# RWKV stage on 64x64 blocks of the array, unrolled, with state steps and the next block's Gram products between the levels

## The chip, the cores and the metric

The kernel runs on one core of a Trainium2 chip. The metric is the device time of one execution in microseconds; the median of 3 runs of the kernel before is 1163.83 us.

The engines are TensorE (PE in the profile; its weight loads are PEld), VectorE (DVE), ScalarE (ACT), GpSimd (POOL) and SyncE (SP), which issues the loads. SBUF is the working memory of 128 partitions, PSUM has 8 banks (ps0 to ps7) of 512 float32 a partition.

## The reference, cut to what matters

One layer of a hybrid decoder on 512 tokens of width 1024: a token mixer with three groups of heads (RWKV-7, forgetting attention, stick-breaking attention), a cross-attention into 256 memory tokens, and a SwiGLU feed-forward part. The change touches only the RWKV-7 group: 6 heads of 64.

```python
def _rwkv7_scan(r, w, k, v, a, b):
    # S_t = S_{t-1}(diag(w_t) + a_t b_t^T) + v_t k_t^T, y_t = S_t r_t
    def step(S, inp):
        r_t, w_t, k_t, v_t, a_t, b_t = inp
        Sa = jnp.einsum('bhij,bhj->bhi', S, a_t)
        S = S * w_t[:, :, None, :] + Sa[..., None] * b_t[:, :, None, :] + v_t[..., None] * k_t[:, :, None, :]
        return S, jnp.einsum('bhij,bhj->bhi', S, r_t)
...
    y = _rwkv7_scan(r4, hs(decay), k4, v4, -kk, kk * a4.astype(jnp.float32))
```

Everything here is float32.

## The kernel before, in words

The kernel is written engine by engine: one instruction stream each, in the order of the code, with semaphores between them. Nothing schedules it. The stages follow each other: input projection (with weights split into a high and a low part, w_hi and w_lo, by GpSimd), the two kinds of attention, then the RWKV stage, the output projection, memory attention and feed-forward.

The RWKV stage doesn't walk token by token. It works in chunks of 64 tokens (CHUNK), two chunks in a block of 128, and four blocks, called turns (NT = 4). The 6 heads lie as 3 pairs c (APAIRS), the two heads g of a pair on partitions 0 to 63 and 64 to 127. In a turn:

- PRE (pre_bk, pre_r, pre_bkh, pre_a, L1505 to L1529) makes the decayed inputs AR (a and r), BK (b and k) and BKh from exponentials E (ScalarE, L1321).
- Four transposes on TensorE (L1066) bring a, b, k and v to tokens on partitions; ScalarE copies them out (L1331).
- Gram products: L1072 (b with a and r, into G1), L1079 (the lower part for Tm), L1085 (k with a and r, into G2). They are made for 128 x 128 tokens at once; the mask gram_mask clears what lies between the two chunks. VectorE masks them (L1541, L1557), adds ident (L1549, L1563) and makes the first inverse TT (L1564).
- L1091 makes the product of G2 and V for the right-hand side RHS.
- Five levels (LEVELS = 2, 4, 8, 16, 32) double the blocks of a triangular inverse: X = G1 with Tm (L1101), masked by VectorE with levm (L1574), then new Tm (L1108) and new TT (L1112), copied out by ScalarE (L1342). Each is a 128 x 128 product for each head, of which half is zero. The heads go in two groups of three, with banks of their own.
- TT times RHS gives WU (L1120, copy L1346). Then GT (L1125), the transfer matrices of both chunks (L1131, L1135, L1136), the state St (L1142, additions L1582 and L1590), the outputs (L1147, L1148, L1154) with the state laid out block-diagonally in Sbd (ScalarE, L1355).

Three turns run in a loop on each engine (Fori), the fourth is written out. A turn's state and outputs end before the next turn's transposes. Behind the stage come the head sums of the group norm (L1168) and the output projection. The masks are made by GpSimd at the kernel's start, between the splits of the first weight panels (L547, L551).

Of the kernel before, what the change touches and what calls it, by code (L numbers as in the profile page):

```python
# [12 lines left out]
P = 128  # L13
# [47 lines left out]
RW_STEPS = 7  # L61
RW_PRE = 6
# [21 lines left out]
def hybrid_block(nc, x, mem, norm_mix_pre, norm_mix_post, w_in, shift_mu, rwkv_w0, rwkv_w_up, rwkv_a0, rwkv_a_up,  # L84
# [4 lines left out]
    with ctx:  # L89
# [49 lines left out]
        grams = sb("gram_mask", [P, 2 * P], where=mix)  # L139
        lowm = sb("lowm", [P, P], where=mix)  # L140
        lowmT = sb("lowmT", [P, P], where=mix)
        levm = sb("levm", [P, len(LEVELS), P], where=mix)
        stack_id = sb("stack_id", [P, HD], where=mix)
# [38 lines left out]
        Rs = sb("Rs", [P, APAIRS, P], where=rw)  # L182
        ends = sb("ends", [P, 2, APAIRS, 1], where=rw)
        Vt = sb("Vt", [P, APAIRS, P], where=rw)
        Dg = sb("Dg", [P, 2, APAIRS, HD], where=rw)
        AR = sb("AR", [P, APAIRS, 2, P], where=rw)
        BK = sb("BK", [P, 2, APAIRS, P], where=rw)
        BKh = sb("BKh", [P, 2, APAIRS, P], where=rw)
        tokBK = sb("tokBK", [P, 2, AH, HD], where=rw)
        tokV = sb("tokV", [P, AH, HD], where=rw)  # L190
        G1 = sb("G1", [P, AH, 2 * P], where=rw)
        G2 = sb("G2", [P, AH, 2 * P], where=rw)
        Tm = sb("Tm", [P, AH, P], where=rw)
        TT = sb("TT", [P, AH, P], where=rw)
        X = sb("X", [P, AH, P], where=rw)
        RHS = sb("RHS", [P, AH, P], where=rw)
        WU = Tm
        GT = sb("GT", [P, APAIRS, P], where=rw)
        PT = sb("PT", [P, 2, APAIRS, P], where=rw)
        QS = sb("QS", [P, 2, APAIRS, HD], where=rw)  # L200
        St = sb("St", [P, 3, APAIRS, HD], where=rw)
        Sbd = sb("Sbd", [P, 2, APAIRS, P], where=rw)
# [261 lines left out]
        def _(sp_eng):  # L464
# [62 lines left out]
        def _(pool):  # L527
# [34 lines left out]
            fill(grams[:, :], 1.0)  # L562
            gv = grams[:, :].rearrange("p (a b j) -> p a b j", a=2, b=2)
            keep(gv[:, 0], [[CHUNK, 2], [1, CHUNK]], 0, -1, ALU.is_gt)
            keep(gv[:, 1], [[CHUNK, 2], [1, CHUNK]], 0, -1, ALU.is_ge)
            keep(gv, [[0, 2], [-CHUNK, 2], [0, CHUNK]], 0, 1, ALU.is_ge)
            fill(lowm[:, :], 0.0)
            keep(lowm[:, 0:P:2], [[-2, P // 2]], -1, 1, ALU.not_equal, 1.0)
            fill(lowmT[:, :], 0.0)
            keep(lowmT[:, :], [[-1, P]], 0, 1, ALU.not_equal, 1.0)  # L570
            keep(lowmT[:, 1:P:2], [[-2, P // 2]], 0, 1, ALU.not_equal, 1.0)
            fill(levm[:, :, :], 1.0)
            for n, m in enumerate(LEVELS):
# [3 lines left out]
                nb = P // (2 * m)  # L577
                v = levm[:, n, :].rearrange("p (b j) -> p b j", b=nb)
# [3 lines left out]
                keep(levm[:, n, :], [[-1, P]], 0, 1, ALU.not_equal, 1.0)  # L582
            for p in (2, 3):
                split(p, p % 2, p // 2)
            fill(stack_id[:, :], 0.0)
            keep(stack_id[:, :], [[-1, HD]], 0, 1, ALU.not_equal, 1.0)
            keep(stack_id[:, :], [[-1, HD]], -HD, 1, ALU.not_equal, 1.0)
# [47 lines left out]
        def level_steps(n, g, which):  # L635

            last = len(LEVELS) - 1
            if n < last:
                return 4 * n + 2 * g + which
            return 4 * n + g + 1  # L640
        N_TE = level_steps(len(LEVELS) - 1, 1, 2)
# [259 lines left out]
        def _(pe):  # L901
# [255 lines left out]
            with pe.Fori(0, NT - 1) as i:  # L1157
                rwkv_turn(i)
# [514 lines left out]
```

## Time and profile before

| | |
|---|---|
| median of 3 runs | 1163.83 us (1161.96 to 1168.35) |
| the profiled execution's span | 1160.8 us |
| PE, DVE, ACT, POOL busy in the span | 92%, 36%, 24%, 42% |
| RWKV stage, 314.6 to 498.1 us | 183.5 us |
| mean granted TensorE clock | 0.972 |

Busy time is the share in which an engine had an instruction under way. Matmuls overlap in the array, so a busy TensorE is not one at its peak; how closely records follow each other tells more. In a timeline a row can stand for several instructions (x10): its first number is the first start, its second the time until the last has ended. In brackets is how long the engine stood idle before it, and whose work ended that. The granted clock is 1.00 at 2.4 GHz and 0.50 at 1.2 GHz.

### The profile page before, as it was taken

The numbers are of one execution on the slowest core, as the hardware profiler recorded it, in microseconds if no ns is written. First come the engines' busy times: TensorE is split into PE (matmuls) and PEld (weight loads), VectorE is DVE, ScalarE is ACT, GpSimd is POOL, SyncE is SP. The second block draws the span as 40 slices with busy tenths as digits, with TensorE's granted clock in tenths as the row PEclk, the third lists the DMA queues.
The fourth block names the chain that finished last, engine by engine and source line by source line (L and its number), as shares of the span: only waits on it lengthen the run. The fifth ranks groups of instructions, "written<-read, shape, count | busy, mean of one in ns | idle before, by whom it ended". The sixth has DMA issues, their size and how long they took to land.

```text
span 1160.8 us, 14862 instructions
## 1 busy us (share of the span) xinstructions
PE 1069.9 (92%) x5717; PEld 861.7 (74%) x5717; DVE 416.5 (36%) x658; ACT 278.3 (24%) x575; POOL 487.2 (42%) x328
## 2 busy tenths in 40 slices
PE   6999997999998998999778988979999999999995
PEld 6788864555587887967766854878888888888884
DVE  4572036453354354262651033053333333320002
ACT  4111253445332332332311143132111111100101
POOL 7966633000000000027675620634666666666562
PEclk9999998999998999999999999989999999999998
DMA  7334211000000000003434310222333333322232
GB/s 214 90 91 107 76 51 57 1 1 1 1 1 1 0 0 0 2 19 109 145 119 136 91 55 1 87 59 74 107 91 91 107 91 91 108 91 91 91 98 83
DMA packets 101931, 79.16 MB, mean 68 GB/s; under 512 B 2656, under 2 KB 87936, under 8 KB 101888
## 3 DMA queue, kind: packets, MB, share of 16 engines
q1 hardware_dynamic: 100592, 73.85, 21.4%
q10 hardware_dynamic: 1296, 4.72, 1.2%
q8 instruction: 30, 0.49, 0.2%
q14 instruction: 13, 0.11, 0.0%
HBM read 76.46 MB, written 2.10 MB: 68 GB/s over the span
## 4 chain that ended last, share of the span: by engine, by line
PE 79%; DVE 9%; ACT 4%; POOL 3%; DMA 2%; issue 2%; DVEq 0%; ACTq 0%; POOLq 0%; SPq 0%
PE ps L425 11%; PE ps L426 11%; PE ps L427 11%; PE ps L455 7%; PE ps L457 7%; PE ps L456 7%; PE ps L1101 3%; PE ps L1112 2%; PE ps L1108 2%; PE ps L989 2%; PE ps L1027 2%; POOL w_lo L551 2%; PE ps L964 1%; DMA raw<-in_mem_wkv 1%; PE ps L696 1%
## 5 line engine op out<-in xcount | busy, mean ns | idle before, releaser
L547 POOL TENSOR_SCALAR w_hi<-raw 128x1024 fp32r<-128x1024 f32 (+2 forms) x135 | 153.0, 1133 | 637.4 <-PE ps L457 454.4
L551 POOL TENSOR_TENSOR w_lo<-raw,w_hi 128x1024 fp32r<-128x1024 f32 (+2 forms) x135 | 314.8, 2332 | 11.2
L425 PE MATMUL ps<-act_hi,w_hi 128*128 128x512 f32 (+1 forms) x632 | 236.9, 375 | 5.5 <-POOL w_lo L551 4.9
L426 PE MATMUL ps<-act_lo,w_hi 128*128 128x512 f32 (+1 forms) x632 | 235.8, 373 | 0.0
L427 PE MATMUL ps<-act_hi,w_lo 128*128 128x512 f32 (+1 forms) x632 | 235.7, 373 | 0.0
L425 PEld LDWEIGHTS ps<-act_hi,w_hi 128*128 128x128 f32 x632 | 119.1, 189 | 28.3 <-POOL w_lo L551 3.5
L427 PEld LDWEIGHTS ps<-act_hi,w_lo 128*128 128x128 f32 x632 | 119.1, 188 | 21.0
L426 PEld LDWEIGHTS ps<-act_lo,w_hi 128*128 128x128 f32 x632 | 119.1, 189 | 20.4
L393 DVE TENSOR_TENSOR ybuf<-ps,gain 128x512 f32<-128x512 f32 x24 | 16.4, 692 | 162.4 <-ACT junk_f L374 117.0
L455 PE MATMUL ps<-w_hi,act_hi 128*128 128x512 f32 (+2 forms) x192 | 71.4, 372 | 2.4 <-DVE act_lo L824 1.4
L457 PE MATMUL ps<-w_hi,act_lo 128*128 128x512 f32 (+2 forms) x192 | 69.8, 363 | 0.0
L456 PE MATMUL ps<-w_lo,act_hi 128*128 128x512 f32 (+2 forms) x192 | 69.8, 363 | 0.0
L457 PE MATMUL ps<-w_hi,a_lo 128*128 128x512 f32 x176 | 69.6, 396 | 0.0
L456 PE MATMUL ps<-w_lo,a_hi 128*128 128x512 f32 x176 | 69.6, 395 | 0.0
L455 PE MATMUL ps<-w_hi,a_hi 128*128 128x512 f32 x176 | 69.6, 395 | 0.0
L886 DVE TENSOR_TENSOR a_lo<-ftmp,a_hi 128x512 f32 (+1 forms) x22 | 56.5, 2570 | 19.6 <-ACT a_hi L868 19.6
L884 DVE TENSOR_TENSOR ftmp<-ps,ftmp 128x512 f32<-128x512 f32 x22 | 15.2, 692 | 88.2 <-PE ps L427 88.2
L455 PEld LDWEIGHTS ps<-w_hi,act_hi 128*128 128x128 f32 x192 | 36.2, 189 | 9.4 <-DVE act_lo L824 2.2
L868 ACT ACTIVATE a_hi<-ftmp 128x512 f32 (+1 forms) x22 | 14.0, 634 | 122.0 <-DVE ftmp L884 122.0
L456 PEld LDWEIGHTS ps<-w_lo,act_hi 128*128 128x128 f32 x192 | 36.2, 188 | 5.7 <-issue 0.7
L457 PEld LDWEIGHTS ps<-w_hi,act_lo 128*128 128x128 f32 x192 | 36.2, 188 | 5.1
L456 PEld LDWEIGHTS ps<-w_lo,a_hi 128*128 128x128 f32 x176 | 33.1, 188 | 8.1
(280 smaller groups left out, 1608.0 us busy)
## 6 DMA issues: line engine op xcount, KB each, us to landing
raw<-in_ffn_w_gu SPq DMA_DIRECT2D x44, 512.0 KB, 3.8
raw<-in_ffn_w_down SPq DMA_DIRECT2D x22, 512.0 KB, 3.7
raw<-in_w_in SPq DMA_DIRECT2D x21, 512.0 KB, 3.8
raw<-in_mem_wkv SPq DMA_DIRECT2D x16, 512.0 KB, 3.8
raw<-in_w_out SPq DMA_DIRECT2D x8, 512.0 KB, 3.7
raw<-in_mem_wq SPq DMA_DIRECT2D x8, 512.0 KB, 3.8
raw<-in_mem_wo SPq DMA_DIRECT2D x8, 512.0 KB, 3.7
xt<-in_x SPq DMA_DIRECT2D x4, 512.0 KB, 7.3
```

What stands on the lines that cost most here:

```text
L425: nc.tensor.matmul(o, hi, a_hi_[:, k, at:at + n], start=(k == 0), stop=False)
L426: nc.tensor.matmul(o, hi, a_lo_[:, k, at:at + n], start=False, stop=False)
L427: last = nc.tensor.matmul(o, lo, a_hi_[:, k, at:at + n], start=False, stop=(k == KT - 1))
L455: nc.tensor.matmul(o, xh, hi, start=(nth == 0 and kk == 0), stop=False)
L456: nc.tensor.matmul(o, xh, lo, start=False, stop=False)
L457: last = nc.tensor.matmul(o, xl, hi, start=False, stop=(nth == pairs - 1 and kk == 1))
L547: nc.gpsimd.tensor_scalar(w_hi[slot][:, 0:n], raw[slot][:, 0:n], 1.0, 1.0, ALU.mult, ALU.mult)\
L551: nc.gpsimd.tensor_tensor(w_lo[slot][:, 0:m], raw[slot][:, 0:m], w_hi[slot][:, 0:m].bitcast(F32), ALU.subtract).then_inc(sig("panel_split" ...
L886: V.tensor_tensor(a_lo[:, bass.ds(f, 1), :], ftmp[:, 2 + b, :].unsqueeze(1), a_hi[:, bass.ds(f, 1), :].bitcast(F32), ALU.subtract).then_in ...
L989: mm(ps[bank][:, 0:NJ[j]], qk[half(h), 2 * APAIRS + CH // 2 + h // 2, P * j:P * j + P], qk[half(h), 2 * APAIRS + h // 2, P * j:T], start=T ...
L1027: last = mm(ps[b][:, P * (j2 - j):NJ[j]], (ntri if j2 == j else nones)[:, :], sp[h % 2][:, OJ[j2]:OJ[j2] + NJ[j2]], start=False, stop=(j2 ...
L1101: last = mm(ps[g][:, P * c:P * c + P], G1[:, 3 * g + c, 0:P], Tm[:, 3 * g + c, :], start=True, stop=True)
```

## The change

The RWKV stage is written anew on all three engines, with the same arithmetic in the same type:

- All products are made for each chunk apart, 64 x 64, with chunk 0 on partitions 0 to 63 and chunk 1 on 64 to 127. G1, G2, Tm, TT and X shrink from 128 to 64 columns for each head, and nothing between chunks is computed. In each product the matmuls alternate between the two chunks (or the two heads of a pair), so that neighbours use different quarters of the array.
- The six heads of a level go as one group: one mask on VectorE and one copy for Tm and for TT on ScalarE, each of 384 columns, where there were two.
- The state is kept as 64 x 64 for each head (St0 to St3), so the block-diagonal copies Sbd and PT and their additions go. PQ takes the transfer matrices and what is added to the state in one VectorE operation for each chunk.
- The state steps and outputs of turn i stand between the levels of turn i + 1. The Gram products of turn i + 1 stand in level 4 of turn i. The transposes stand one by one in the levels 0 to 3. AR, BK, G1, G2, tokV and ends have two buffers.
- The four turns are written out without a loop.
- The masks are 64 wide, made by GpSimd on 64 partitions in one tile, chunk_masks, and copied to the other 64 by a DMA on SP's queue, ahead of the loads of the Q panels.

```diff
+            def by_chunk(bank, lhs, rhs, width, heads=range(AH)):
+                for n, hh in enumerate(heads):
+                    for ch in range(2):
+                        last = mm(ps[bank][half(ch), width * n:width * n + width], lhs[half(ch), hh, :], rhs[half(ch), hh, :],
+                                  start=True, stop=True)
+                return last
...
+            def turn_pe(i):
+                more = i + 1 < NT
+                level_x(i, 0)
+                toks(0, i)
+                if i:
+                    pe.wait_ge(sig("rw_pq"), 2 * i)
...
+                    state_step(i - 1, 0)
+                level_t(i, 0)
+                pe.wait_ge(sig("rw_tok"), 4 * i + 1)
+                gram(i, 0, 3, 1, "rw_g2m")
...
+            def transfers(i):
+                dve.wait_ge(sig("rw_dg"), 2 * i + 3)
                 for ch in range(2):
+                    dve.wait_ge(sig("rw_pqm"), 2 * i + ch + 1)
+                    V.tensor_tensor(PQ[:, ch], ps[2 + 2 * ch][:, 0:AW].rearrange("p (a c n) -> p a c n", a=2, c=APAIRS),
+                                    Dg[:, ch], ALU.add).then_inc(sig("rw_pq"), 1)
...
+            sp_eng.wait_ge(sig("half_masks"), 1)
+            sp_eng.dma_start(chunk_masks[CHUNK:P], chunk_masks[0:CHUNK]).then_inc(sig("masks_both"), 16)
```

TensorE in the levels, before. A row is a run of equal matmuls, with the bank that it writes and its size; L1101 is X, L1108 and L1112 are the new Tm and TT:

```order
L1101 MATMUL ps0<-Tm,G1 128x128 x3
...
L1101 MATMUL ps1<-Tm,G1 128x128 x3
...
L1108 MATMUL ps2<-X,TT 128x128 x3
L1112 MATMUL ps4<-TT,X 128x128 x3
...
L1108 MATMUL ps3<-X,TT 128x128 x3
L1112 MATMUL ps5<-TT,X 128x128 x3
```

And in the change, levels 1 and 2 of turn 1 (L1075 is by_chunk; L1104 a state step and L1113, L1116, L1122 the outputs of turn 0; L1058 a Gram product, L1050 a transpose):

```order
L1075 MATMUL ps0<-Tm,G11 64x64 x12
L1104 MATMUL ps4<-St1,PQ 64x64 x6
L1058 MATMUL ps3<-AR1,BK1 64x128 x6
L1075 MATMUL ps1<-X,TT 64x64 x12
L1075 MATMUL ps2<-TT,X 64x64 x12
L1050 MATMUL ps4<-ident,AR1 128x128 x3
...
L1075 MATMUL ps3<-tokV1,G21 64x64 x12
L1113 MATMUL ps4<-G10,WU 64x64 x2
L1116 MATMUL ps4<-G20,tokV0 64x64 x2
```

Two groups of three heads became one group of 12 small matmuls, and between X and the T products now stands work of other steps and of the turn before.

VectorE from a turn's end on, before (PT, GT, St, Y are the transfer, output and state additions):

```order
L1582 TENSOR_TENSOR PT<-ps2,Dg 64x3x64 x2
L1582 TENSOR_TENSOR PT<-ps3,Dg 64x3x64 x2
L1586 TENSOR_TENSOR GT<-ps7,Rs 128x384
L1590 TENSOR_TENSOR St<-ps4,QS 128x192 x2
...
L1595 TENSOR_TENSOR Y<-ps6,Y 128x3x128
...
L1537 COPY St<-St 128x192
L1541 TENSOR_TENSOR G1<-ps4,gram_mask 128x512
```

And in the change, from level 4 of turn 0 to level 0 of turn 1:

```order
L1636 TENSOR_TENSOR G11<-ps3,chunk_masks 128x384
L1648 TENSOR_TENSOR Tm<-ps4,chunk_masks 128x192
L1648 TENSOR_TENSOR Tm<-ps3,chunk_masks 128x192
L1651 TENSOR_TENSOR Tm<-Tm,chunk_masks 128x384
L1653 TENSOR_TENSOR G11<-G11,chunk_masks 128x6x64
L1712 COPY WU<-ps1 128x384
L1658 TENSOR_TENSOR TT<-G11,chunk_masks 128x384
L1682 TENSOR_TENSOR PQ<-ps2,Dg 128x384
L1682 TENSOR_TENSOR PQ<-ps4,Dg 128x384
L1687 TENSOR_TENSOR GT<-ps0,AR0 128x3x64
L1687 TENSOR_TENSOR GT<-ps1,AR0 128x3x64
L1667 TENSOR_TENSOR X<-ps0,chunk_masks 128x384
```

The next turn's masks and additions now stand ahead of this turn's WU, PQ and GT, and the state addition comes behind the next turn's first X.

## Rows read from the trace of the kernel before

**Rows 1.** The page's first part: busy time, share and instructions of each engine.

```profile
PE 1069.9 (92%) x5717; PEld 861.7 (74%) x5717; DVE 416.5 (36%) x658; ACT 278.3 (24%) x575; POOL 487.2 (42%) x328
```

**Rows 2.** Windows, turns two and four, and all four's sum; columns: us, busy by engine, clock.

```profile
360.48:407.65 47.17, 43.09 (x374) 40.33 (x372) 20.39 (x42) 16.19 (x36) 0.00 (x0) 0.92 0.00 0
...
453.14:498.10 44.96, 39.98 (x373) 36.85 (x370) 17.98 (x36) 15.83 (x33) 0.00 (x0) 1.00 0.00 1
sum 183.50, PE 165.74 PEld 153.81 DVE 80.19 ACT 64.62 POOL 0.00; mean PE 41.44 PEld 38.45 DVE 20.05 ACT 16.16 POOL 0.00
```

**Rows 3.** The chain, one level: start us, us, engine and line.

```profile
378.11 1.51 PE ps L1101 x12
...
380.36 0.67 PE ps L1112 x6
...
382.37 1.51 PE ps L1101 x12
```

**Rows 4.** Groups by shape in turn two: busy us, mean ns of one.

```profile
L1574 DVE TENSOR_TENSOR X<-ps,levm 128x384 f32<-128x384 f32 x10 | 5.6, 558 | 12.5 <-PE ps L1101 12.5
...
L1342 ACT ACTIVATE Tm<-ps 128x384 f32<-128x384 f32 x8 | 3.9, 491 | 7.7 <-PE ps L1108 7.7
...
L1590 DVE TENSOR_TENSOR St<-ps,QS 128x192 f32<-128x192 f32 x2 | 0.7, 352 | 2.1 <-PE ps L1142 2.1
```

**Rows 5.** TensorE's timeline, the transfer matrices in 64x64: start us, us until the last end.

```profile
397.17 0.61 PE L1131 MATMUL ps<-tokBK,Tm 64*64 64x64 f32 x10
397.57 0.22 PE L1135 MATMUL ps<-Tm,tokBK 64*64 64x64 f32 x1
397.62 0.22 PE L1131 MATMUL ps<-tokBK,Tm 64*64 64x64 f32 x1
397.63 0.22 PE L1135 MATMUL ps<-Tm,tokBK 64*64 64x64 f32 x1
397.68 0.22 PE L1131 MATMUL ps<-tokBK,Tm 64*64 64x64 f32 x1
...
397.80 0.28 PE L1135 MATMUL ps<-Tm,tokBK 64*64 64x64 f32 x2
397.92 0.28 PE L1136 MATMUL ps<-tokV,tokBK 64*64 64x64 f32 x2
...
400.07 0.28 PE L1136 MATMUL ps<-tokV,tokBK 64*64 64x64 f32 x2
...
400.29 0.88 PE L1142 MATMUL ps<-St,PT 128*128 128x64 f32 x6
```

**Rows 6.** The timeline of turn two, handoffs to TensorE; idle time in brackets.

```profile
367.94 1.35 DVE L1541 TENSOR_TENSOR G<-ps,gram_mask 128x256 f32<-128x256 f32 x3
...
369.34 2.83 PE L1091 MATMUL ps<-tokV,G 128*128 128x64 f32 x12 [2.00 <-DVE G L1541]
...
395.55 0.49 ACT L1346 ACTIVATE Tm<-ps 128x384 f32<-128x384 f32 x1 [0.35 <-PE ps L1120]
...
396.10 1.14 PE L1125 MATMUL ps<-G,Tm 128*64 128x128 f32 x12 [0.58 <-ACT Tm L1346]
```

**Rows 7.** Windows, three stretches with their granted clock (the last number but two).

```profile
348.60:355.40 6.80, 6.22 (x103) 5.74 (x103) 2.06 (x6) 1.15 (x3) 0.00 (x0) 1.00 0.02 5
365.70:369.10 3.40, 1.64 (x14) 1.15 (x10) 2.84 (x7) 0.00 (x0) 0.00 (x0) 1.00 0.00 0
369.10:376.00 6.90, 6.66 (x31) 6.66 (x32) 4.60 (x10) 2.25 (x5) 0.00 (x0) 0.51 0.00 0
```

**Rows 8.** GpSimd's timeline in the opening.

```profile
36.05 1.19 POOL L534 TENSOR_SCALAR_AFFINE_SELECT stack_id<-stack_id 128x64 f32<-128x64 f32 x2
```

**Rows 9.** The chain in the opening.

```profile
42.82 0.51 POOL w_lo L551
...
52.27 2.41 POOL w_lo L551
54.73 0.50 PE ps L425
```

More of the change, by code:

```diff
@@ L60 @@
 SMALL_LOADS = 16 * 12
-RW_STEPS = 7
-RW_PRE = 6
 def panel_run(eng, first, count, unroll, body):
@@ L138, in hybrid_block @@
         reset = sb("reset", [P, T], where=mix)
[L139 to L143, printed above, removed]
+        chunk_masks = sb("chunk_masks", [P, 2 + 2 + len(LEVELS) + 1, CHUNK], where=mix)
+        grams = chunk_masks[:, 0:2, :]
+        lowm, lowmT = chunk_masks[:, 2, :], chunk_masks[:, 3, :]
+        levm = [chunk_masks[:, 4 + n, :] for n in range(len(LEVELS))]
+        eye = chunk_masks[:, 4 + len(LEVELS), :]
         att = ExitStack()
@@ new lines, in gram, with lower @@
+            def gram(i, g, bank, b, sem):
+                for c in range(APAIRS):
+                    for ch in range(2):
+                        now = slice(CHUNK * ch, CHUNK * ch + CHUNK)
+                        last = mm(ps[bank][half(ch), P * c:P * c + P].rearrange("p (a n) -> p a n", a=2),
+                                  BK[i % 2][half(g), b, c, now], AR[i % 2][half(g), c, :, now], start=True, stop=True)
+                last.then_inc(sig(sem), 1)
+            def lower(i, g, bank):
+                for c in range(APAIRS):
+                    for ch in range(2):
+                        now = slice(CHUNK * ch, CHUNK * ch + CHUNK)
+                        last = mm(ps[bank][half(ch), CHUNK * c:CHUNK * c + CHUNK], AR[i % 2][half(g), c, 0, now],
+                                  BK[i % 2][half(g), 0, c, now], start=True, stop=True)
+                last.then_inc(sig("rw_nm"), 1)
@@ new lines, in level_t, with state_step @@
+            def level_t(i, n):
+                pe.wait_ge(sig("rw_x"), len(LEVELS) * i + n + 1)
+                if n == 0:
+                    pe.wait_ge(sig("rw_t2"), i + 1)
+                else:
+                    pe.wait_ge(sig("rw_te"), TURN_TE * i + 2 * n)
+                if n < LAST:
+                    by_chunk(1, TT, X, CHUNK).then_inc(sig("rw_tm"), 1)
+                by_chunk(2, X, TT, CHUNK).then_inc(sig("rw_tm"), 1)
+            def state_step(i, ch):
+                n = 2 * i + ch
+                for c in range(APAIRS):
+                    for g in range(2):
+                        last = mm(ps[4][half(g), HD * c:HD * c + HD], PQ[half(g), ch, 0, c, :], St[n % 4][half(g), c, :],
+                                  start=True, stop=True)
+                last.then_inc(sig("rw_sm"), 1)
@@ L1157, in _ @@
-            with pe.Fori(0, NT - 1) as i:
-                rwkv_turn(i)
-            rwkv_turn(NT - 1)
+            pe.wait_ge(sig("masks_both"), 16)
+            pe.wait_ge(sig("rw_in"), 1)
+            gram(0, 0, 4, 0, "rw_g1m")
+            gram(0, 1, 3, 0, "rw_g1m")
+            pe.wait_ge(sig("rw_g1"), 1)
+            lower(0, 0, 4)
+            pe.wait_ge(sig("rw_g1"), 2)
+            lower(0, 1, 3)
+            for i in range(NT):
+                turn_pe(i)
+            pe.wait_ge(sig("rw_pq"), 2 * NT)
@@ L1364, in _ @@
+            act.wait_ge(sig("stick_pv"), CH)
+            for which in range(3):
+                decay(0, which)
+            for i in range(NT):
+                turn_act(i)
+            y_out(NT - 1, 0)
+            y_out(NT - 1, 1)
             for c in range(APAIRS):
```

555 lines of the change are left out of this document (294 added, 261 removed).

## The prediction

> **What bounds the kernel now.** I read first the busy line of the page: TensorE works in 92% of the span [rows 1]. The change touches one stretch, the RWKV stage, which is four turns (blocks of 128 tokens). The windows, one per turn, give its size: from 314.6 to 498.1 us, 183.5 us in all, 45.0 to 47.2 us a turn, and in a turn TensorE is busy 41.4 us, VectorE 20.1, ScalarE 16.2 and GpSimd not at all [rows 2]. So the stage is paced by TensorE. The chain shows it at its finest: one level of the triangular inverse is nothing but matmul pieces, 1.51 us for the X product and then pieces of about 0.67 us without a gap, 4.26 us from one level's start to the next [rows 3]. That is 36 records (6 heads x 3 products, and a float32 matmul leaves two records) at 0.118 us. The masks on VectorE (0.56 us) and the copies on ScalarE (0.49 us) lie beside it [rows 4], because the six heads are worked as two groups of three, and one group's matmuls run while the other's result is masked or copied. Everything behind 498.1 us hangs on the end of this stage.
>
> **What a small tile costs.** The new code does nearly all of this on 64x64 quarters of the array, so its price per record is the term that decides. The old kernel has one place of that kind [rows 5]. Where one quarter alone is fed, records start 0.058 us apart: two of L1135 from 397.80, then L1136 at 397.92. Where two quarters have work, they run at once: L1135 and L1131 start at 397.57, 397.62, 397.63 and 397.68, 0.03 us from one to the next, each line's records keeping their 0.058. The whole block of 72 records takes 3.12 us (397.17 to 400.29), 0.043 each, since the old order feeds one quarter six or twelve records in a row. The second quarter joins only when about three records of the first are left, so the array looks only a few records ahead. The new order gives one matmul to one quarter and the next to the other, within that reach. I take 0.029 us a record, with bounds 0.0146 (four quarters at once) and 0.058 (none at once). A record that streams 128 columns takes twice that, 0.056 on two quarters. Full 128x128 transposes stay at 0.112, as six records in 0.67 us [rows 3]. Between a quarter-mode record and a full-mode one lie 0.17 us (last L1136 at 400.13, L1142 at 400.29) in place of 0.06: 0.1 us for each change of mode.
>
> **One level, new.** X product: 24 records x 0.029 = 0.70 us, 0.22 for the last to land [rows 5], 0.05 to wake VectorE, 0.56 for the mask (same 384 columns as before, but now for all six heads), 0.1 to restart TensorE: the T products start at 1.63. Their first half again takes 0.92, 0.05, then the ScalarE copy 0.49 and 0.06: the next X product can start at 3.15. Wake-ups are from the rows in which an engine waited: 0.05 us from VectorE's end (367.94 + 1.35) to L1091 at 369.34, and 0.06 from ScalarE's 396.04 to L1125 at 396.10 [rows 6]. TensorE issues 72 records x 0.029 = 2.1 us of that. The level is no longer TensorE's own pace but a round trip over three engines, with about 0.9 us free between X and T. Into that hole and behind T the change puts other work. Behind T it is not hidden, since T ends at 3.03.
>
> **One full turn, new,** by the order of the rows of after. TensorE's work: 288 matmuls on 64 columns = 576 records x 0.029 = 16.8 us; 36 on 128 columns = 72 records x 0.056 = 4.0; 12 transposes = 24 x 0.112 = 2.7; 8 changes of mode = 0.8. Sum 24.3 us, against 41.4 busy now. By levels, start to start: levels 0 and 1 with transposes, a state step and a Gram half each 4.2; level 2, which holds the product with V and both output groups, 5.9, with two waits of 0.25 on its own results; level 3 with two transposes 4.0; level 4 with Gram, lower part, solution, transfer matrices and GT up to the next level 0: 10.0. Sum 28.3 us. So about 4.0 us remain in which TensorE waits: the masks and copies that the fill doesn't cover, 0.9 for the copy of WU, and some 1.3 at the turn's end, where GT's two additions stand ahead of the next X product. VectorE has 21 operations x 0.56 and 8 x 0.35 [rows 4], 14.6 us, ScalarE some 10: neither becomes the bound. The old tail of each turn (state steps, their copies into Sbd, the output products, each behind the other) now lies under the next turn's levels, and the wait of 2.00 us for the Gram masks ahead of L1091 [rows 6] goes, because the next block's Gram products are made before this block's end.
>
> **The whole stage.** Prologue (first block's Gram and lower products with four masks and two additions, nothing to hide them) 4.4 us. Turn 0 has no earlier state to carry, 96 records and a wait less, but then shows some mask waits: 25.0. Turns 1 and 2: 56.6. The last turn and what follows it (two state steps with a VectorE addition each, and two output groups, all in series) 32.6. Sum 118.6 us.
>
> **The clock.** The granted clock falls to 0.50 (1.2 GHz) at 369.1, behind a stretch in which TensorE was busy for 1.64 us of 3.40 [rows 7]. From 348.6 to 355.4 it worked on parts of the array only and kept 1.00, 2.4 GHz [rows 7], so small tiles alone don't lower it. In the new turn the gaps at the end (0.9 and 1.3 us, close together) are of that kind. At half clock a turn of 28.3 us would be 51 (24.3 doubles, less the mode changes), so each microsecond at half costs 0.45. I put in three falls of 3.4 us, 4.6 us in all; as in the stage of now, they may be more or fewer. **Stage 123.2 us, a gain of 60.3.**
>
> **The opening.** The masks are half as wide and made on half of the partitions, and stack_id is gone. Most of that is hidden: GpSimd then waits for the panel to be used. But stack_id's selects took 1.19 us of GpSimd at 36.05 [rows 8], between two splits of panels for which TensorE later waited: the chain goes over w_lo for 0.51 us at 42.82, and again over w_lo at 52.27 up to L425 at 54.73 [rows 9]. With 1.19 us less ahead both waits go or shrink: the first is worth its 0.51, the second what is left of the 1.19 at most; I take 1.0 us for both. The new copy of the masks to the other half of the partitions (160 KB) stands on SP's queue ahead of the Q panels; behind it wait only loads that a full slot holds back, and its readers wait at 311 us. The 512 KB loads land in 3.8 us on the page. I cost it at nothing; if SP's queue stood still for that whole time once, 4 us would be lost at most, and nothing reads a gain from it.
>
> **Sum.** 60.3 + 1.0 = 61.3 us. Against the profiled span of 1160.8 that gives 1099.5; the median of the runs is 3.0 us above the span, so 1102.5 us. A difference of 0.5% (5.8 us) is about what a measurement of this kernel can tell from none.
>
> By the Trainium skill, page "TensorE: Matmul & The Clock Gate", section "Part 3: Packing small matmuls", matmuls on tiles of different groups start about 4 ns apart, so all four quarters would run at once. The trace never shows more than two for long. By that rule the 96 records of the transfer matrices and GT, which alone use four quarters, would take 1.4 us in place of 2.8 in a turn, and the sum would be 1096.9.
>
> **Rivals.**
> (a) The four quarters do run at once, or the waits that I count at the turn's end are covered: 96 records x 0.0146 less in four turns, 5.6 us, and no falls of the clock, 4.6: 1092.
> (b) The clock stays low. If half of the new stage runs at half clock, the stage is 118.6/(1 - 0.45 x 0.5) = 153 us and the kernel 1132. For it: TensorE now stops for a mask or a copy in every level. Against it: the gaps of a level are under 0.2 us with the fill, and the Gram and small-tile stretches of now kept 1.00.
> (c) The other side: quarters on opposite corners don't run at once when fed in turn, and a record takes 0.058. Then a turn has 576 x 0.058 + 72 x 0.112 + 3.5 = 45 us of TensorE work, and with some 3 us of waits 48; the stage is 4.4 + 44 + 96 + 46 = 190 us and with the falls of the clock 195, and the kernel 1174, slower than now. It decides from 0.055 us a record on (118.6 grows by 2.5 for each 0.001). Against it: the interleaved starts at 397.57 to 397.68 and a mean of 0.043 even in the unfavourable order. The same end is reached if over 80% of the stage is at half clock.
> (d) Unrolling: the turn is now straight code of some 336 matmuls, read once. If instruction loads lag behind the short records by 1 to 1.5 us a few times a turn, 5 to 20 us are lost: 1108 to 1122. The three turns of the old loop read the same code again, so the trace says little for or against.
>
> **Chances.** My forecast with its own range 1094 to 1112: 0.60. (a) 0.10, (b) at 1112 to 1150: 0.13, (d) 0.10, (c) 0.06, and 0.01 for within 0.5%. The range 1088 to 1132 takes in (a), (d), the nearer half of (b) and both ends of the tile price that still give two quarters at once. Faster by over 0.5%: 0.93; within: 0.01 plus the tail of (b), 0.02; slower: 0.05.
>
> **What the profile would show.** Right: the stage (from the first Gram product to the first of the head sums) in 118 to 128 us; four turns near 28; the X and T products with 0.029 us from record to record; masks at 0.56 and copies at 0.49 us as before; VectorE's mask waiting for L1075, and TensorE waiting for the mask only briefly; clock at 1.00 but for a few short falls at the turns' ends; behind the stage everything as now, 60 us earlier. Wrong: records 0.058 apart within a product; long stretches at 0.50; gaps on TensorE that end with no releaser; or a level 4 of over 12 us, which would mean that VectorE's queue (Gram masks, additions, the copy of WU, then the transfers) is the turn's real path.

## The result, and the profile after

The changed kernel takes 1084.63 us (median of 4 runs, 1082.1 to 1088.38), the kernel before on the same chip 1162.89 (1160.64 to 1168.35). The ratio is 0.932, with a 95% interval of 0.928 to 0.936. The forecast was 1102.5 with 1088 to 1132: right in direction, and too small a gain, 61.3 us where the profiled spans differ by 77.1 (1160.8 and 1083.7). Of the 17.9 us between 1102.5 and 1084.6 the spans account for 15.8; the other 2.1 come from the median, which lies 0.9 us above the profiled span and not 3.0.

The page after, first part: busy us, share of the span, instructions.

```profile
PE 1000.1 (92%) x6869; PEld 795.2 (73%) x6869; DVE 393.0 (36%) x609; ACT 250.3 (23%) x511; POOL 481.0 (44%) x325
```

TensorE works 70 us less [rows 1], with a fifth more records. Windows of the stage after, in the columns of [rows 2]: the prologue, turn 0, turn 1 (turn 2 reads the same, 24.88), the last turn with its tail up to the first product of the head sums, and the two stretches at half clock.

```profile
314.06:318.15 4.09, 2.19 (x50) 1.77 (x49) 2.79 (x7) 0.00 (x0) 0.00 (x0) 0.93 0.00 0
318.15:343.18 25.03, 22.70 (x565) 20.79 (x565) 13.19 (x29) 8.56 (x18) 0.00 (x0) 0.87 0.01 3
343.18:368.05 24.87, 22.41 (x660) 20.79 (x661) 13.26 (x30) 9.23 (x20) 0.00 (x0) 1.00 0.02 4
...
392.93:423.74 30.81, 26.24 (x709) 23.54 (x709) 8.84 (x21) 8.70 (x20) 0.00 (x0) 0.94 0.01 3
317.60:324.40 6.80, 6.25 (x91) 5.80 (x92) 1.61 (x4) 1.88 (x4) 0.00 (x0) 0.50 0.01 2
420.00:426.80 6.80, 6.25 (x56) 4.22 (x53) 2.77 (x4) 1.95 (x3) 0.00 (x0) 0.50 0.01 2
```

The stage takes 423.74 - 314.06 = 109.7 us where it took 183.5 [rows 2]: 73.8 us of the 77.1. The forecast was 123.2.

| part of the stage | forecast, us | after, us |
|---|---|---|
| prologue | 4.4 | 4.1 |
| turn 0 | 25.0 | 25.0, of it 6.2 at half clock |
| turns 1 and 2 | 56.6 | 49.75 |
| last turn and tail | 32.6 | 30.8, of it 3.7 at half clock |
| falls of the clock, apart from these | 4.6 | 0 |

Turn 1 by levels, each from its X product to the next level's, in the same columns:

```profile
343.18:346.74 3.56, 3.56 (x97) 3.33 (x99) 0.92 (x2) 1.21 (x3) 0.00 (x0) 1.00 0.00 0
346.74:350.56 3.82, 3.82 (x106) 3.59 (x102) 2.87 (x6) 1.53 (x4) 0.00 (x0) 1.00 0.03 6
350.56:356.07 5.51, 5.38 (x170) 5.10 (x171) 2.58 (x7) 2.82 (x7) 0.00 (x0) 1.00 0.01 3
356.07:359.61 3.54, 3.36 (x84) 2.82 (x80) 1.02 (x2) 2.08 (x5) 0.00 (x0) 1.00 0.02 5
359.61:368.05 8.44, 6.29 (x217) 5.96 (x217) 5.87 (x13) 1.58 (x4) 0.00 (x0) 1.00 0.02 5
```

The forecast had 4.2, 4.2, 5.9, 4.0 and 10.0: every level is shorter, most of all the last. In levels 0 and 1 TensorE has no idle time at all; nearly all of its 2.46 us of waiting in the turn lie in level 4. The timeline after shows level 0 and the end of level 4 (start us, us until the last end, then engine, line, count; idle time in brackets):

```profile
343.18 0.92 PE L1075 MATMUL ps<-Tm,G 64*64 64x64 f32 x24 [1.44 <-DVE GT L1687]
344.02 0.55 PE L1050 MATMUL ps<-ident,z 128*128 128x128 f32 x3
...
344.50 0.56 PE L1104 MATMUL ps<-St,PQ 64*64 64x64 f32 x12
344.90 0.87 PE L1075 MATMUL ps<-X,TT 64*64 64x64 f32 x24
345.60 0.80 PE L1075 MATMUL ps<-TT,X 64*64 64x64 f32 x21
...
346.19 0.32 PE L1058 MATMUL ps<-AR,BK 64*64 64x128 f32 x1
346.19 0.28 PE L1075 MATMUL ps<-TT,X 64*64 64x64 f32 x3
...
364.98 0.34 PE L1141 MATMUL ps<-tokBK,WU 64*64 64x64 f32 x8 [0.71 <-issue]
365.12 0.33 PE L1145 MATMUL ps<-WU,tokBK 64*64 64x64 f32 x8
365.23 0.33 PE L1149 MATMUL ps<-tokV,tokBK 64*64 64x64 f32 x8
365.35 0.33 PE L1141 MATMUL ps<-tokBK,WU 64*64 64x64 f32 x8
...
366.35 1.02 DVE L1682 TENSOR_TENSOR PQ<-ps,Dg 128x384 f32<-128x384 f32 x2 [1.01 <-PE ps L1149]
367.29 0.61 DVE L1687 TENSOR_TENSOR GT<-ps,AR 128x192 f32<-128x192 f32 x2
368.05 0.92 PE L1075 MATMUL ps<-Tm,G 64*64 64x64 f32 x24 [1.44 <-DVE GT L1687]
```

Three things stand here that the forecast had otherwise. The transfer matrices (L1141, L1145, L1149), whose matmuls go to the four quarters in turn, start a group of eight records every 0.117 us: 0.0146 a record, so all four quarters work at once (a record of one quarter alone comes every 0.058 us [rows 5]). Three transposes (L1050) leave three records, not six, and the next work starts 0.48 us behind them. And the last records of one product run among the first of the next on another quarter (L1058 and L1075 both at 346.19). What was forecast right: a level product's 24 records take 0.70 us before the next one's start (344.90 to 345.60, 0.029 a record on two quarters), masks 0.56 and copies 0.49. TensorE leaves 660 records in the turn, where the forecast had 672: the 12 are the transposes.

### The profile page after: what moved, and what is told of

It is laid out like the page before. It is cut to its first block, busy times and chain, and to the rows that moved or that the text cites. A ratio compares the mean times of both kernels' runs of the same rounds, so it can differ in the third digit from the quotient of the medians.

```text
span 1083.7 us, 16803 instructions
## 1 busy us (share of the span) xinstructions
PE 1000.1 (92%) x6869; PEld 795.2 (73%) x6869; DVE 393.0 (36%) x609; ACT 250.3 (23%) x511; POOL 481.0 (44%) x325
## 4 chain that ended last, share of the span: by engine, by line
PE 80%; DVE 9%; ACT 3%; POOL 3%; DMA 2%; issue 2%; DVEq 0%; POOLq 0%; ACTq 0%; SPq 0%
PE ps L419 12%; PE ps L421 12%; PE ps L420 12%; PE ps L449 7%; PE ps L450 7%; PE ps L451 7%; PE ps L1075 5%; PE ps L1015 2%; PE ps L977 2%; POOL w_lo L547 2%; PE ps L952 1%; DMA raw<-in_mem_wkv 1%; PE ps L684 1%; PE ps L970 1%; PE ps L942 1%
## 5 line engine op out<-in xcount | busy, mean ns | idle before, releaser
L543 POOL TENSOR_SCALAR w_hi<-raw 128x1024 fp32r<-128x1024 f32 (+2 forms) x135 | 150.4, 1114 | 566.7 <-PE ps L451 380.3
```

Of the source, the lines that this page charges most:

```text
L543: nc.gpsimd.tensor_scalar(w_hi[slot][:, 0:n], raw[slot][:, 0:n], 1.0, 1.0, ALU.mult, ALU.mult)\
```

## The experiments

Each kernel ran on one chip with the kernel before. The medians of before lie between 1162.6 and 1167.4 on these, and the changed kernel on one of them once more gave 1083.67. I compare small differences by the spans and the turns in the traces, since the intervals of the ratios are 0.6 to 0.9% wide.

**1. Four quarters in the old kernel.** The kernel before, with its 36 transfer-matrix products (L1131 to L1136) issued to the four quarters in turn.

```diff
-for ch in range(2): for g, c, hh in HH: mm(... WU, tokBK ...)
-                    for g, c, hh in HH: mm(... tokBK, WU ...); mm(... tokBK, tokV ...)
+for c in range(APAIRS):
+    for ch, g in quads: mm(... WU, tokBK ...)
+    for ch, g in quads: mm(... tokBK, WU ...)
+    for ch, g in quads: mm(... tokBK, tokV ...)
```

> The old kernel with one edit: the 72 records of the transfer matrices (L1131, L1135, L1136) are issued so that neighbours use the four different quarters of the array. Theory A (all four quarters run at once, as 0.014 us a record in the changed kernel suggests): the block takes about 1.05 us in place of 3.12, so some 2 us a turn and 8 us in all are gained at most, less what then waits for ScalarE's copy of QS: 1155 to 1158 us. Theory B (two at a time, as the forecast had it): 2.1 us, 1 us a turn: about 1159. Theory C (the order makes no difference): 3.1 us and 1163.

Measured: 1168.2 us, ratio 1.003 (0.999 to 1.007). TensorE's timeline of this run:

```profile
397.81 0.34 PE L1132 MATMUL ps<-tokBK,Tm 64*64 64x64 f32 x8
397.98 0.30 PE L1139 MATMUL ps<-Tm,tokBK 64*64 64x64 f32 x8
...
398.80 0.30 PE L1141 MATMUL ps<-tokV,tokBK 64*64 64x64 f32 x8
400.43 0.77 PE L1148 MATMUL ps<-St,PT 128*128 128x64 f32 x5 [1.34 <-DVE PT L1588]
```

The block that took 3.12 us [rows 5] now takes 1.1: from the second group on, eight records start every 0.117 us, 0.0146 a record. So the price is a matter of the order of issue, and it holds in the old kernel too. The time missed the 1155 to 1158 us of theory A. Of the 2 us a turn, 0.5 are left: TensorE then waits 1.34 us for VectorE's additions of PT (L1588), and these for ScalarE's copy QS, so that the state step starts 2.62 us behind the block's start where it started 3.12 behind it. And this profile's stage has more of the half clock, 0.92 on average where the kernel before has 0.96:

```profile
315.11:503.96 188.85, 165.90 (x1489) 153.62 (x1489) 80.22 (x165) 64.73 (x141) 0.00 (x0) 0.92 0.00 1
```

That is more than the 0.5 us a turn can make good. Whether the new wait brings these falls on or only this execution had them, one profile doesn't tell; in the medians no difference is seen.

**2. One quarter after the other.** The changed kernel with the two loops of its product helper swapped, so that the heads of one chunk are issued before those of the other.

```diff
-for n, hh in enumerate(heads):
-    for ch in range(2):
+for ch in range(2):
+    for n, hh in enumerate(heads):
```

> The changed kernel with one edit: in by_chunk (all level products, the product with V, and WU) all matmuls of chunk 0 are issued before those of chunk 1, so that 6 to 12 records in a row go to the same quarter. Theory A (what pays is that neighbours use different quarters, and the array looks only a few records ahead): a product of 24 records takes about 0.58 us for the first quarter less an overlap of about three records, 1.2 us in place of 0.7; 14 such products and four of twice the width add 0.5 to 0.6 us each, of which a part lies in holes: 4 to 7 us a turn, 1102 to 1112 us. Theory B (the array reorders deeply, the order does not matter): 1085.

Measured: 1126.81 us, ratio 0.966 (0.960 to 0.972). Windows of turn 0 and turn 1, and TensorE's timeline:

```profile
318.57:362.08 43.51, 41.14 (x565) 38.89 (x565) 13.14 (x29) 8.61 (x18) 0.00 (x0) 0.57 0.01 2
362.08:393.54 31.46, 28.80 (x661) 26.93 (x661) 13.13 (x30) 9.24 (x20) 0.00 (x0) 1.00 0.01 3
...
362.08 1.40 PE L1075 MATMUL ps<-Tm,G 64*64 64x64 f32 x24 [1.44 <-DVE GT L1687]
363.41 0.55 PE L1050 MATMUL ps<-ident,z 128*128 128x128 f32 x3
```

The 24 records of a product take 1.33 us, 0.055 each, and a full turn 31.5 us in place of 24.9. The same instructions in another order cost 6.6 us a turn, within the 4 to 7 of theory A; so with 12 records in a row to one quarter the second quarter doesn't join in. The time is beyond its 1102 to 1112, because in turn 0 the granted clock was 0.57 on average and the turn took 43.5 us; the turn that follows has 1.00. All four runs have a mean clock of 0.956 to 0.963, the changed kernel's four 0.973 to 0.981, so this is no single execution's matter. This run is the nearest to rival (b), a stage at half clock for long.

**3. The transfer matrices by chunk.** Within a chunk only two quarters alternate in the 96 records of L1141 to L1156, as the forecast had assumed.

```diff
-for c in range(APAIRS):
-    for ch, g in TILES: mm(...)
+for ch in range(2):
+    for c in range(APAIRS):
+        for g in range(2): mm(...)
```

> The changed kernel, with the 96 records of PQ and GT issued chunk by chunk, so that only two quarters of the array alternate in place of four. Everything else as in the changed kernel. Theory A (what the trace after shows: four quarters at once, 0.0146 us a record, the term that the prediction had at 0.029): the block of 96 records takes 2.8 us in place of 1.4. VectorE can take PQ of chunk 0 at the same moment as before, so of the 1.4 us only 0.5 to 1.4 us a turn reach the path: time 1087 to 1090 us. Rival B (the order of these records plays no part, and the gain beyond the forecast came from the transposes and the overlap alone): the block stays at 1.4 us and the time at 1084.6. Rival C (the block is longer but TensorE waits for VectorE's transfers anyway): block 2.8 us, wait before the next X product shorter by as much, time 1084.6.

Measured: 1087.84 us (6 runs), ratio 0.932 (0.929 to 0.936). The turn, and its level 4:

```profile
346.56:371.79 25.23, 23.29 (x660) 21.66 (x661) 13.35 (x30) 9.22 (x20) 0.00 (x0) 1.00 0.02 4
363.00:371.79 8.79, 7.16 (x217) 6.83 (x217) 5.96 (x13) 1.58 (x4) 0.00 (x0) 1.00 0.02 5
```

TensorE's busy time grows by 0.88 us, the turn by 0.36. The block of 96 goes from 1.41 us to 2.28, first start to last, and not to 2.8: inside a chunk four records start every 0.117 us (0.029 each), but where the records of one chunk border on the other's, both pairs of quarters run together. Between theories A and C: most of the longer block is taken out of TensorE's wait for GT, which falls from 1.44 to 0.92 us, because chunk 0 is complete as early as before and VectorE begins with it. The median is 3 to 4 us above the changed kernel's, but 1.4 us are what four turns show; the rest is not explained by this edit.

**4. Transposes as products.** Each of the 12 transposes of a turn as a matmul with the identity, which leaves two records.

```diff
-last = nc.tensor.transpose(ps[...], src[:, c, :], ident[:, :])
+last = mm(ps[...], src[:, c, :], ident[:, :], start=True, stop=True)
```

> The changed kernel, with each of the 12 transposes of a turn written as a product with the identity. The trace shows one record for a transpose and two for a product of float32; the prediction had counted two for a transpose (24 records of 0.112 us, 2.7 us a turn). Theory A (the mis-sized term is real and on the path, since in levels 0 to 3 TensorE's queue ends the level): 24 records of 128 columns in place of 12, some 1.3 us a turn more, 1088 to 1089 us. Rival B (the transposes lie in TensorE's waits for masks and copies, so the term was mis-sized without weight): 24 records all the same, time 1084 to 1085. By the run with each mask done twice, which came out as if every mask were on the chain, B or something between is the likelier: 1084 to 1086.5 us.

Measured: 1090.36 us (6 runs), ratio 0.937 (0.934 to 0.940). Levels 0 and 3 of turn 1 (level 1 has 4.21, level 2 5.50, level 4 8.44), then the turn:

```profile
344.10:348.06 3.96, 3.96 (x101) 3.77 (x103) 0.92 (x2) 1.22 (x3) 0.00 (x0) 1.00 0.00 0
...
357.77:361.84 4.07, 4.07 (x90) 3.70 (x86) 1.02 (x2) 2.21 (x5) 0.00 (x0) 1.00 0.00 0
...
344.10:370.28 26.18, 23.90 (x673) 22.55 (x673) 13.26 (x30) 9.25 (x20) 0.00 (x0) 1.00 0.01 4
```

The turn is 1.31 us longer: 0.40 and 0.39 in levels 0 and 1 with three transposes each, 0.53 in level 3 with six, nothing in the two levels without. Theory A holds, against the odds that I gave it: the transposes are on the path nearly in full (12 further records at 0.112 would be 1.34 us), and counting two records for one was worth 1.3 us a turn.

**5. Each level's mask twice.**

```diff
+V.tensor_tensor(X, ps0, levm[n], mult).then_inc("rw_x_first")
+dve.wait_ge("rw_x_first", ...)
 V.tensor_tensor(X, ps0, levm[n], mult).then_inc("rw_x")
```

> The changed kernel, with VectorE's mask of each level done twice, so that each of the 20 masks takes some 0.5 us more. What it tells: how much of a level is the chain of product, mask, product, copy, and how much is TensorE's own filling work. Theory A (levels are still bound by TensorE's queue in all places where state steps, outputs or Gram work stand between the products, so that only levels 1 and 4 see the mask): one to 1.5 us a turn, 1089 to 1091 us. Rival B (the chain through VectorE and ScalarE sets each level's length, the fillings are all hidden): 20 x 0.5 = 10 us, 1094 to 1096 us. Near 1085: the masks are hidden in every level.

Measured: 1094.41 us, ratio 0.938 (0.933 to 0.943). The turn goes from 24.87 to 27.02 us, and the levels to 4.05, 4.35, 5.50, 4.15 and 8.97. The row of level 2:

```profile
355.70:361.20 5.50, 5.37 (x169) 5.09 (x170) 3.14 (x8) 2.82 (x7) 0.00 (x0) 1.00 0.01 3
```

Rival B, but for level 2: every mask's 0.5 us shows in full (0.49, 0.53, 0.61 and 0.53 us), only level 2, where TensorE has the product with V and both output groups, hides it. With experiment 4 this says that in levels 0, 1 and 3 the round trip over VectorE and TensorE's own queue end at nearly the same moment: whichever is made longer sets the level.

**6 and 7. Placing.** State steps and outputs at the end of their own turn; and, in another kernel, the next block's Gram and lower products behind the transfers.

```diff
 turn_pe(i), first kernel:
-if i: state_step(i - 1, 0) ... state_step(i - 1, 1) ... outputs(i - 1, 0) ... outputs(i - 1, 1)
+solved(i); state_step(i, 0); state_step(i, 1); outputs(i, 0); outputs(i, 1)
 second kernel:
-gram(i + 1, ...); level_t(i, 4); lower(i + 1, ...); solved(i)
+level_t(i, 4); solved(i); gram(i + 1, ...); lower(i + 1, ...)
```

> The changed kernel with the state steps and outputs of a turn back at its own end, ahead of the next turn's first level. Theory A (they are hidden work: 72 + 24 records in holes): at the end of each of the first three turns the serial chain of the last turn's end appears (about 5 to 6 us from the transfers to the outputs), and 2.5 to 3 us of matmuls leave the levels: 3 us a turn, 1092 to 1096 us. Theory B (the gain comes from the small tiles alone and the placing is worth nothing): 1085.

> The changed kernel with the next block's Gram and lower products, their masks and additions behind the turn's transfer matrices in place of level 4. Theory A: each of the three turns gets the prologue's 4 us of unhidden work at its end and loses about 1.5 to 2 us of it in level 4: 2 to 3 us a turn, 1091 to 1094 us. Theory B (placing is worth nothing): 1085.

Measured: 1095.41 us (ratio 0.938, 0.932 to 0.943) and 1104.29 us (0.945, 0.939 to 0.952). A full turn of each, then levels 0 and 4 of the second:

```profile
352.51:380.65 28.14, 25.30 (x665) 22.78 (x664) 13.36 (x30) 9.22 (x20) 0.00 (x0) 0.92 0.02 4
...
350.38:380.98 30.60, 25.53 (x660) 22.97 (x660) 13.38 (x31) 9.22 (x20) 0.00 (x0) 0.89 0.01 3
350.38:356.10 5.72, 5.72 (x97) 5.27 (x99) 1.45 (x3) 1.21 (x3) 0.00 (x0) 0.57 0.00 0
368.98:380.98 12.00, 7.25 (x217) 6.19 (x216) 5.45 (x13) 1.58 (x4) 0.00 (x0) 0.92 0.01 3
```

With the clock that goes with it, placing the state work between the levels is worth 3.3 to 3.8 us a turn, the Gram work 5.7. The first kernel too has the half clock in the turn shown, some 4 us of it by its mean of 0.92; the row is the fall that begins at the turn's end:

```profile
379.00:385.90 6.90, 6.84 (x109) 6.21 (x107) 0.56 (x1) 1.68 (x5) 0.00 (x0) 0.51 0.01 2
```

At the 0.44 us that a microsecond at half clock costs in the second kernel (below) this would be some 2 of the 3.3 us, an estimate: no kernel with the state work at the turn's end ran at full clock. The second kernel has TensorE busy for 7.25 of 12.00 us in level 4, and from 1.8 us before that level's end the clock falls to 0.50 for 6.8 us in each turn: level 0 takes 5.72 us for work that takes 3.56 at full clock.

**8. The same placing, TensorE kept busy.** The second kernel of these, with eleven filling matmuls of 512 columns a turn in its waits, into a bank that nobody reads.

```diff
+keep_warm(7, 3) ... keep_warm(7, 2) ... keep_warm(7, 1) ... keep_warm(7, 5)
```

> The kernel with the next block's Gram work behind the transfers (1104.3 us, half clock for 6.8 us in every turn), and in its waits at the turn's end filling matmuls on a bank that nobody reads (11 of 512 columns a turn). It is the pair to that kernel: same placing, other clock. Theory A (of the 6 us a turn that the placing cost, some 3 are the half clock that its waits bring on): the half-clock stretches of the turns go and the time is 1092 to 1097 us. Rival B (the placing costs all of it by itself and the clock only goes along): 1102 to 1108 us, with the half-clock stretches gone. Rival C (fillers do not keep the clock): stretches stay, 1104 us or more.

Measured: 1097.93 us, ratio 0.941 (0.936 to 0.946). The turn, its level 0 and its level 4:

```profile
346.93:375.95 29.02, 26.50 (x683) 23.75 (x683) 13.37 (x31) 9.23 (x20) 0.00 (x0) 1.00 0.01 3
346.93:350.50 3.57, 3.57 (x98) 3.33 (x100) 1.45 (x3) 1.22 (x3) 0.00 (x0) 1.00 0.02 5
363.37:375.95 12.58, 10.37 (x240) 8.92 (x239) 5.45 (x13) 1.58 (x4) 0.00 (x0) 1.00 0.01 3
```

6.4 us of the 19.7 come back, nearest to theory A. Level 0 is at 3.57 again (2.15 us less), level 4 is 0.58 us longer with the fillers, what they cost less what its own end gains from the full clock. So of the 5.7 us a turn at least 2.15 are the clock and at most 3.6 the placing by itself (29.02 - 24.87 - 0.58).

**9. Fillers in the changed kernel.** Ten filling matmuls in the prologue and seven in the tail; with it ran the changed kernel itself as base.

```diff
 gram(0, 0, 4, 0, "rw_g1m"); gram(0, 1, 3, 0, "rw_g1m")
+keep_warm(7, 2) ... keep_warm(7, 1) ... keep_warm(7, 5)
 for i in range(NT): turn_pe(i)
+keep_warm(7, 3) ... keep_warm(7, 2) ... keep_warm(7, 2)
```

> The changed kernel once more, unaltered, on the chip on which the three below run, as their base. Expected: 1083 to 1086 us.

> The changed kernel with filling matmuls on a bank that nobody reads: ten of 512 columns in the waits of the prologue and seven in the tail, where the granted clock fell to half (317.6 to 324.4 and 420.0 to 426.8 us after). Theory A (the two falls follow from TensorE's idle time there, and cost what their columns at half clock cost, about 0.45 us per us): both stretches go, turn 0 falls from 25.0 by up to 2 us, the tail by one to 2 us: 1081 to 1083 us. Rival B (turn 0's and the tail's chains hang on VectorE and ScalarE, so the clock costs nothing): 1084 to 1085, stretches gone. Rival C (the fall comes all the same, moved): 1084 to 1086.

Measured: 1083.67 us (1081.04 to 1088.31) for the base and 1082.55 (1079.94 to 1084.79) with the fillers, ratios 0.931 and 0.930. Turn 0, and the last turn with the tail:

```profile
321.85:344.31 22.46, 19.95 (x564) 18.18 (x565) 13.18 (x29) 8.55 (x18) 0.00 (x0) 1.00 0.01 4
394.07:423.86 29.79, 26.95 (x723) 24.18 (x723) 8.83 (x21) 8.68 (x20) 0.00 (x0) 1.00 0.01 3
```

Both falls are gone. Turn 0 is 2.6 us shorter, the end 1.0; the prologue is 0.65 us longer with its fillers (4.73), and the whole stage is 106.7 us in place of 109.8 for the base. In the medians 1.1 us of it are seen, less than their scatter, so the total gain of the fillers is not settled; the size of the two falls in the stage is. Nor is one profile proof that the fillers took the falls away. Of the ten profiles whose prologue and tail have no fillers, nine have a fall at the prologue and seven one in the tail, but that of experiment 10 has neither; the two with fillers have none.

**10 and 11. A better version.** The wait of 1.44 us at each turn's head is a matter of order: the next X product needs neither PQ nor GT, only the bank that GT used. The kernel gives GT banks of its own, issues the next turn's X product in the wait for WU's copies, masks it ahead of the transfers, and puts the first state step behind the first T products. The second kernel adds the fillers of experiment 9 and issues the last outputs' products of WU, V and G ahead of the last state steps.

```diff
 solved(i):  by_chunk(1, TT, RHS, ...)
+            if i + 1 < NT: level_x(i + 1, 0)
             ... PQ, then GT:
-            mm(ps[ch] ..., WU, G1)
+            mm(ps[5 + ch] ..., WU, G1)
 VectorE:    first_inverse(i + 1)
+            level_mask(i + 1, 0)
             transfers(i)
```

> The changed kernel with the next turn's first product and its mask drawn ahead of the transfers: X of level 0 is issued in TensorE's wait for WU's copies, GT goes to banks of its own, VectorE masks X before it takes PQ and GT, and the state step of chunk 0 comes after the first T products. If the wait of 1.4 us before X, the product's 0.8 and the mask's 0.6 at the head of turns 1 to 3 come out of the chain and the transfers' 2 us on VectorE are in level 0 in their place only in part: 2 to 2.5 us for each of three turns, 1077 to 1079 us. Rival (the transfers' time on VectorE delays state_out and the Gram masks by as much, and level 0 gets longer by what the head got shorter): 1083 to 1086 us.

> The early X product and the fillers together, with the last turn's outputs split so that their products of WU, V and G go ahead of the state steps in the last tail. If the shares add: early X 6 to 7.5 us, outputs 1 to 1.5, clock 0 to 3: 1073 to 1077 us. Rival (as above, the transfers delay level 0): 1081 to 1084 us.

Measured: 1077.43 us (1076.48 to 1083.16), ratio 0.927 (0.923 to 0.931), and 1075.17 us (1072.74 to 1076.07), ratio 0.923 (0.919 to 0.927). A full turn of the first (level 0, now with the transfers in it, has 4.97 us and level 4 has 4.79), its last turn and tail, and those of the second:

```profile
339.77:362.40 22.63, 22.19 (x661) 20.65 (x661) 13.26 (x31) 9.21 (x20) 0.00 (x0) 1.00 0.02 4
...
385.02:416.08 31.06, 26.49 (x804) 23.87 (x804) 11.33 (x27) 8.67 (x20) 0.00 (x0) 1.00 0.01 4
...
386.06:415.66 29.60, 26.51 (x808) 24.13 (x808) 11.33 (x27) 8.69 (x20) 0.00 (x0) 1.00 0.02 4
```

A turn is 2.24 us shorter, as expected, and TensorE waits 0.44 us in it in place of 2.46. What is left is TensorE's own work. Both profiles are at full clock in the whole stage, so they also show the last outputs' split by itself: the last turn and tail take 31.06 us in the first kernel and 29.60 in the second, 1.46 less (1 to 1.5 were expected), while the fillers cost the second 0.65 in the prologue. The second kernel is 8.5 us faster than the changed one on the same chip, and their runs don't overlap.

## Why the prediction was wrong in size, point by point

**The stage was seen rightly as the place of the gain** (73.8 of 77.1 us), and so was what a level becomes: a round trip of product, mask, product and copy, with other work in the hole. Experiment 5 shows the first, experiments 6 and 7 the second. The price of 0.029 us a record on two quarters held. What failed are two terms of the turn's sum, both of them prices of TensorE's records: the 96 records of the transfer matrices and GT, and the 12 transposes. The clock's term was too large as well.

**96 records at 0.029, two quarters at a time: a step that failed.** It was read from [rows 5], where the old order feeds one quarter six or twelve records in a row. That the array looks only a few records ahead was right for such an order: experiment 2 has 0.055 a record with twelve in a row. But it doesn't follow that two quarters are the most. Those rows show what this order does, not what the array can do. With the records given to four quarters in turn, both kernels show 0.0146 us. The rule that I had set beside it from the Trainium skill (page "TensorE: Matmul & The Clock Gate", section "Part 3: Packing small matmuls") was right on this: all four work at once, and the block of 96 takes 1.4 us. The starts themselves lie 6 to 10 ns apart within a group of four records, not 4, and 35 ns pass before the next group. The bound of 0.0146 was in my text and I gave it a tenth of the chance. In level 4 the 72 records ahead of PQ end 72 x 0.0146 = 1.05 us earlier than forecast: 4.2 us for four turns. This is worked out, and no run shows it: experiment 3 measures 0.36 us a turn for its order, 1.4 in all, since that order gives chunk 0 to VectorE as soon as before and lengthens the block by 0.87 us in place of 1.4.

**"12 transposes = 24 x 0.112": the other step, mis-sized by double.** I carried over from the products of float32 that each leaves two records. The count could have been read before: L1066 makes 48 transposes there, twelve a turn, and the trace of before groups them so (count and ns of one):

```profile
L1066 PE MATMUL ps<-ident,BKh x24: 272/273/421, 315.0 to 453.9; 128*128 128x128 f32 x24
L1066 PE MATMUL ps<-ident,AR x12: 272/276/421, 314.6 to 453.2; 128*128 128x128 f32 x12
L1066 PE MATMUL ps<-ident,Vt x12: 272/273/421, 315.6 to 454.2; 128*128 128x128 f32 x12
```

That is 48 records for 48 transposes. Experiment 4 measures the term at 1.3 us a turn, 5.2 in all.

**The sum of levels took each product as ended before the next began.** The trace after shows the records of two products interleaved (346.19). Of the 28.3 - 24.9 = 3.4 us a turn, 1.3 and 1.05 are named above, which leaves 1.1. The rows by level say where: 0.24 in level 0, none in level 1, 0.39 in level 2, -0.07 in level 3 and 0.51 in level 4. In level 2 it is the waits: 0.5 us were counted, and TensorE idles 0.13. For levels 0 and 4 I put it down to the overlap and to rounding up; that is argued, not measured, since no run took the overlap alone away.

**The clock.** Three falls at the turns' ends were booked, 4.6 us. None came there; one came with the prologue's waits and one with the tail's, 2.6 and 1.0 us by experiment 9. The condition named (a wait at the turn's end, with the clock falling with it) was real for longer waits: experiment 7 has it in every turn, with TensorE idle for 4.75 us in level 4 where the changed kernel idles 2.15. So the mechanism was right and its place wrong: 4.6 against some 3 to 3.6. That the sum came near is luck in part, for which falls a stage has differs between executions of the same code (experiment 9). The forecast's row for small tiles at full clock, 348.6 to 355.4 [rows 7], also holds six records on the full array (L1142); turn 1 after is the better witness. The price of 0.45 us for each us at half clock held roughly, 2.6 us for 6.2 in turn 0 (0.41) and 2.15 for 4.9 behind level 4 of experiment 7 (0.44).

**The whole stage at full clock** was forecast at 118.6 and measures 106.7 with the fillers. Of the 11.9 us too much, 5.2 are the transposes, measured; up to 4.2 the four quarters, worked out; and at least 2.5 the rest, whose cause is open but for the waits of level 2. With 1.6 less for the clock than booked that makes the 13.5 between 123.2 and 109.7.

**The opening: 0.4 us where 1.0 was forecast.** After the change GpSimd's chain in the opening ends here (start us, us), where [rows 9] had 54.73:

```profile
54.34 0.50 PE ps L419
```

The 1.19 us that GpSimd saves [rows 8] bring 0.39 (in the twelve profiles of kernels with this opening the row starts at 54.26 to 54.64, 0.1 to 0.5 us ahead). Between the two panels it now waits 1.29 us for TensorE to give a panel free, and this eats most of them:

```profile
42.94 1.05 POOL L543 TENSOR_SCALAR w_hi<-raw 128x1024 fp32r<-128x1024 f32 x1 [1.29 <-PE ps L421]
```

**Behind the stage** nothing was changed, and the profiles differ by 2.7 us there (662.7 before, 660.0 after). Among the twelve profiles of kernels with the same code as after in that stretch it takes 657.6 to 662.9 us, so this is scatter that the forecast could not have held. The missing 15.8 us are then 13.5 in the stage and 2.7 behind it, less 0.45: before the stage 0.55 us were gained by the profiles (314.61 and 314.06) where 1.0 was forecast. That start scatters too, from 314.1 to 317.7 us over the twelve profiles.

**The rivals.** (a), four quarters at once and no falls, gave 1092 and named the right price of the records; its absence of falls was wrong by some 3 us, and it was still 7 us too slow, 5.2 of them the transposes. (b), a clock that stays low, didn't happen here, but the order of experiment 2 brought it about for a whole turn. (c), quarters that don't run at once, is what the same experiment shows for products fed quarter by quarter: 31.5 us a turn, not the 48 that I gave, since the rest of the turn stays interleaved. (d), instruction loads, isn't seen: in turn 1 only 0.71 us of TensorE's idle time are put down to issue, ahead of L1141, and they stand where it waits for the copies of WU by ScalarE and VectorE (364.32 + 0.56 for the later one).

## What to carry to other kernels

The price of a small-tile matmul is set by the order in which the tiles are fed: 0.058 us a record on one quarter, 0.029 on two, 0.0146 on four in turn. An old order that feeds them in runs shows a mixture and is no bound; take the ideal price as a real candidate and let the consumers decide what it is worth, since in experiment 3 only 0.36 us of 0.88 reached the path. A level between TensorE, VectorE and ScalarE has to be summed with its waits, and a profile of one execution doesn't settle where the clock falls. Count records per operation from the trace, one kind of operation at a time. When a chain over several engines and the queue of the busiest end at the same moment, each microsecond added to either costs a microsecond; what pays then is to issue the head of the next chain into the last wait of this one.

## What I had not expected of the hardware

- Four quarters of the array at once: 0.0146 us from record to record, in both kernels. 0.055 where one quarter was fed for 12 records in a row.
- A transpose of 128x128 float32 leaves one record, a product of the same size two. The doubling costs 0.13 us each in levels 0 and 1 (0.40 us for three) and 0.09 in level 3 (0.53 for six).
- In experiment 2 the granted clock stayed at 0.50 (1.2 GHz) for 37.6 us, with TensorE busy for 37.2 of them, and was 1.00 for the whole of the next two turns on the same kind of work. The window's row:

```profile
318.20:355.80 37.60, 37.23 (x431) 35.44 (x435) 9.25 (x20) 7.62 (x16) 0.00 (x0) 0.50 0.01 2
```

  What kept it down in turn 0 alone, the runs don't tell.
- Work placed in a wait can be worth more than its length: the Gram work takes 4.1 us in the prologue, and leaving it behind the transfers cost 5.7 us a turn, of which at least 2.15 was the half clock that came with the longer wait.
